# Five first slices of 128, 128, 256, 256 and 256 features, rows loaded by ACT at once and turned between the tiles of x, first weights in two blocks and three pairs

## The chip, the cores and the metric

The kernel runs on one NeuronCore of a Trainium2 chip, in fp32. The time is that of one launch on the device in microseconds; the figure for a kernel is the median of its runs. The engines are PE (TensorE, matrix products and transposes), DVE (VectorE), ACT (ScalarE), POOL (GpSimd) and SP (SyncE, which here only issues transfers).

## What is computed

One decoder layer on a sequence of 512 tokens and 1024 features. The change touches its first steps only:

```python
mod = silu(c) @ w_ada + b_ada                  # c: 1024, w_ada: 1024 x 6144
shift1, scale1, gate1, shift2, scale2, gate2 = split(mod, 6)
h = rms_norm(x, norm1_g) * (1 + scale1) + shift1
proj = h @ w_in                                # 1024 -> q, k, v, qi, ki, wi, u_pool, g_attn, g_pool
# then: indexer scores (qi, ki, wi), the 128 best keys of each query, attention with ALiBi over them,
# a causal pooling mixer, both gated and merged, @ w_out, added to x;
# then the second norm, modulated, @ w_up, a causal convolution of width 3 (conv_w, conv_b), silu gate, @ w_down
```

## The kernel before

Every matrix product in fp32 is made of three products of rounded parts: the operand is split into a high part (fp32r) and a low part (the rest), and PE adds high x high, high x low and low x high into one bank of PSUM. ACT makes high parts (`high_parts`, L788), DVE or POOL the low parts of weights (`low_parts`, L1209 on DVE in the first phase, L704 on POOL afterwards). Each engine runs a list written out by hand and waits on semaphores; nothing reorders it.

The first phase needs h transposed (features on partitions), in eight blocks k of 128 features, each 128 x 512 tokens. It goes so:

- SP issues the four tiles of x (L627), eleven small loads of rows (biases, gains, convolution taps, L630 to L637), then in turn for each of four slices of 256 features the part of w_ada for shift1 and scale1 (`load_first`, tiles ada_first0 to 3, four loads of 512 KB each with pieces of 1 KB) and the rows of w_in for the same two blocks k (`load_item`, tiles stage). Then come eight loads ada_row of 512 KB for shift2, and the weights of v.
- ACT loads c, takes silu(c) and then for each tile of tokens the sum of squares and the root (L805, L808). DVE takes the reciprocal and scales x into xn (L1240). PE turns xn in 128 x 128 pieces into all eight banks (L1613). ACT and DVE copy the banks to xT (four each).
- PE then sums slice 0 of mod with matmuls of c against ada_first (`first_sums`, L1627, into the eighth bank OB), ACT copies the four partial rows (L816), PE turns them into columns with matmuls against ones (`first_columns`, L1635), DVE adds the bias from the turned rows (`first_vectors`, L1217 to L1222), makes h of a block (full1, L1252), ACT its high part (L820), DVE its low part (L1229) and the low part of the weights (L1209). The rows and taps are turned on PE in one go between the sums and the columns of slice 0 (L1652 to L1655).
- PE does for each block k seven products of high x high, seven of h's low part and seven of the weights' low part (`first_products`, L1645), into seven banks that stay open over all eight blocks: qi (two), ki and wi (kw), q (four). The sums of the next slice stand behind the first block of a slice and its columns within the second.
- DVE accumulates the eight rows of macc_rows (the shift of the second norm; `mod_row_of`, L1171 and L1174) in two groups: five behind slice 2 and three behind slice 3. Only then come the low parts of qiT and kiT (L1261), which the first products of the indexer on PE wait for (`index_dots`, L1706), and then the indexer sums and fifteen rounds that find the best keys (L1309, L1312), up to kraw (L1351), for which the first attention scores on PE wait (L1827).

Of the kernel before, what the change touches and what calls it, by code (L numbers as in the profile page):

```python
# [62 lines left out]
ROW_LOADS = 11  # L63
# [8 lines left out]
KQ = KD // 2  # L72
THREE = ((0, 0), (0, 1), (1, 0))
# [40 lines left out]
class Schedule:  # L114
# [38 lines left out]
    def first(self):  # L153

        for q in range(KQ):
            self.items.append(("first", "in", (C_Q, C_QI), 2 * q, 2 * q + 2, 1))
            self.last_use.append(None)
            for r in range(2):
                self.units.append((1, r, KS))
                self.house()  # L160
                self.item_of.append(q)
                self.last_use[q] = ("unit", len(self.units))
        for at, name in enumerate(FIRST):
            self.opens(name, "dve", FIRST_BANK[at])
        self.ring = NBANK - 1
# [89 lines left out]
def build_layer(nc, x, c, w_ada, b_ada, norm1_g, w_in, q_norm_g, k_norm_g, w_attn_br, w_pool_grp, pool_scale,  # L255
# [17 lines left out]
    with ExitStack() as ctx:  # L273
# [53 lines left out]
        xn = place("xn", [P, NT, D], F32, hT_at)  # L327
# [3 lines left out]
        ada_first = [arena(f"ada_first{q}", [P, KD, S], F32, (16, 32, 62, 89)[q]) for q in range(KQ)]  # L331
# [78 lines left out]
        rows_in = sem("rows_in")  # L410
        x_in = [sem(f"x_in{t}") for t in range(NT)]
# [4 lines left out]
        ada_in = [[sem(f"ada_in{q}_{half}") for half in range(2)] for q in range(KQ)]  # L416
# [13 lines left out]
        c_t = sem("c_t")  # L430
        c_silu = sem("c_silu")
        c_pad = sem("c_pad")
        x_sum = sem("x_sum")
        x_t = sem("x_t")
        x_kept = [sem("x_kept_even"), sem("x_kept_odd")]
# [155 lines left out]
        def _(sp):  # L591
            def load_item(n):
# [5 lines left out]
                if kind == "first":  # L598
                    for c0, wide, c in FIRST_COLUMNS:
                        sp.dma_start(slot[:, 0:2 * KS].rearrange("p (k n) -> p k n", n=KS)[:, :, c:c + wide],  # L600
# [27 lines left out]
            for r, src in ((V_ADA, b_ada), (V_NORM1, norm1_g), (V_NORM2, norm2_g), (V_POOL, pool_scale)):  # L628
                v = src[0].rearrange("(k p) -> k p", p=P)
                sp.dma_start(rows[r:r + v.shape[0], 0, :], v).then_inc(rows_in, 16)  # L630
            for r, src in ((V_Q, q_norm_g), (V_K, k_norm_g)):
                for half in range(2):
                    sp.dma_start(rows[r:r + 1, 0, half * HD:(half + 1) * HD], src).then_inc(rows_in, 16)
            taps = conv_w[0].rearrange("j (m p) -> (j m) p", p=P)
            sp.dma_start(rows[:, 1, :], taps[0:P, :]).then_inc(rows_in, 16)
            sp.dma_start(rows[0:TAPS * 2 * KF - P, 2, :], taps[P:TAPS * 2 * KF, :]).then_inc(rows_in, 16)
            sp.dma_start(rows[TAPS * 2 * KF - P:(TAPS + 1) * 2 * KF - P, 2, :],  # L637
                          conv_b[0].rearrange("(m p) -> m p", p=P)).then_inc(rows_in, 16)
            def load_row(k):

                if k % 4 == 0:
                    sp.wait_ge(sums_ok, k // 4 + 1)
                sp.dma_start(ada_row[k][:, :], ada[:, k, 3 * D:4 * D]).then_inc(ada_row_in[k], 16)

            for n, item in enumerate(sch.items):
                if n < KQ:
                    load_first(n)
                if n == KQ + 4:
                    sp.wait_ge(sums_ok, KQ - 1)
# [7 lines left out]
                if n == KQ - 1:  # L657
# [115 lines left out]
        def _(act):  # L773
# [29 lines left out]
            for t in range(NT):  # L803
                act.wait_ge(x_in[t], 16)
                me.did(act.activation(junk[:, t % 2, :], xtok[:, t, :], ACT.Square,  # L805
                                      accum_out=tstat[:, 0, t:t + 1]), x_sum)
# [1164 lines left out]
```

## Time and profile before

| what | us |
|---|---|
| median of three runs | 735.16 |
| lowest, highest | 735.04, 736.5 |
| the profiled execution | 735.97 |
| its span, first to last instruction | 734.1 |
| PE busy | 717.5 |
| DVE, ACT, POOL busy | 382.5, 307.7, 299.8 |

The page of the profile gives the busy time of each engine and a chain of the work that ended last. The views used below are: the busy time of each engine in stretches of the span, with the clock granted to TensorE (1.00 is 2.4 GHz, 0.50 is 1.2 GHz) and the share and rate of the DMA engines; the waits; the chain; and the timeline, in which consecutive instructions of one line are merged with their count.

### The profile page before, as it was taken

To read this page: it belongs to the slowest core of one execution; us is meant where nothing else is said; L and a number is where in the kernel's file an instruction comes from. 1 tells how busy PE (TensorE), PEld (TensorE's weight loads), DVE (VectorE), ACT (ScalarE), POOL (GpSimd) and SP (SyncE) were. 2 spreads that over 40 slices of the span, in tenths; PEclk is the share of its full clock that TensorE was granted. 3 is DMA by queue.
4 is the path that set the end of the run, shared out by engine and by line. 5 is a ranking of instruction groups with operands and counts; after the bars stand their busy time and mean duration, and the time that the engine had idled before them with its cause. 6 is when DMAs were issued, how large, how long until landed. Compare 5 with 4: busy or idle time off the path is not lost.

```text
span 734.1 us, 9316 instructions
## 1 busy us (share of the span) xinstructions
PE 717.5 (98%) x3440; PEld 577.4 (79%) x3440; DVE 382.5 (52%) x706; ACT 307.7 (42%) x507; POOL 299.8 (41%) x159
## 2 busy tenths in 40 slices
PE   5899999999999999999999999999999999999997
PEld 3667688877776778887898888887888888888886
DVE  3458899964375506788955444545443432004002
ACT  6316532567577633352636334344334333121120
POOL 1001448826232325574315434434444434435440
PEclk9899999999999999999999999999999999999999
DMA  9993321311231226486095243244243233042401
GB/s 317 357 392 115 108 80 58 115 58 59 69 103 53 64 66 258 164 307 208 1 315 151 81 115 105 68 115 114 58 116 96 76 114 114 31 144 86 144 0 58
DMA packets 87306, 92.73 MB, mean 126 GB/s; under 512 B 2275, under 2 KB 69599, under 8 KB 87263
## 3 DMA queue, kind: packets, MB, share of 16 engines
q1 hardware_dynamic: 84927, 83.23, 35.5%
q10 hardware_dynamic: 2336, 8.92, 3.3%
q8 instruction: 28, 0.46, 0.3%
q14 instruction: 15, 0.12, 0.1%
HBM read 90.05 MB, written 2.10 MB: 126 GB/s over the span
## 4 chain that ended last, share of the span: by engine, by line
PE 81%; DVE 14%; ACT 1%; DMA 1%; SPq 1%; issue 1%; DVEq 0%; ACTq 0%
PE bank L1575 33%; PE bank L1595 21%; PE bank L1584 16%; PE bank L1645 4%; DVE work L1312 3%; DVE top L1309 3%; PE bank L1839 1%; PE bank L1827 1%; PE bank L1807 1%; DMA ada_first<-in_w_ada_dram 1%; PE bank L1627 1%; DVE macc_rows L1174 1%; DVE full L1490 1%; DVE pmean L1343 1%; DVE pmean L1339 1%
## 5 line engine op out<-in xcount | busy, mean ns | idle before, releaser
L704 POOL TENSOR_TENSOR wsplit<-stage,wsplit 128x1024 fp32r<-128x1024 f32 (+1 forms) x113 | 259.3, 2297 | 387.3 <-ACT wsplit L788 328.0
L1575 PE MATMUL bank<-hT,wsplit 128*128 128x512 f32 (+1 forms) x1120 | 257.5, 382 | 0.4 <-DVE hT L1498 0.4
L1575 PEld LDWEIGHTS bank<-hT,wsplit 128*128 128x128 f32 x1120 | 203.0, 188 | 41.9 <-issue 1.7
L788 ACT ACTIVATE wsplit<-stage 128x1024 fp32r<-128x1024 f32 (+2 forms) x121 | 120.0, 994 | 249.8 <-PE bank L1584 165.2
L1584 PE MATMUL bank<-hT,wsplit 128*128 128x512 f32 (+1 forms) x560 | 134.6, 382 | 0.0
L1595 PE MATMUL bank<-wsplit,guT 128*128 128x512 f32 x528 | 119.8, 389 | 0.0
L1584 PEld LDWEIGHTS bank<-hT,wsplit 128*128 128x128 f32 x560 | 101.5, 188 | 19.9 <-POOL wsplit L704 0.3
L1595 PEld LDWEIGHTS bank<-wsplit,guT 128*128 128x128 f32 x528 | 99.1, 188 | 20.6
L1533 DVE SCALAR_TENSOR_TENSOR yb<-bank,conv,yb 128x511 f32<-128x511 f32 (+1 forms) x44 | 33.0, 749 | 65.1 <-ACT yb L1108 64.3
L1533 DVE SCALAR_TENSOR_TENSOR ya<-bank,conv,ya 128x511 f32<-128x511 f32 (+1 forms) x44 | 33.0, 750 | 59.6 <-ACT ya L1108 58.8
L1458 DVE TENSOR_TENSOR tmp_last<-bank,gate_row 128x512 f32<-128x512 f32 x8 | 5.5, 688 | 101.7 <-PE bank L1595 101.7
L1645 PE MATMUL bank<-hT,wsplit 128*128 128x512 f32 x168 | 42.4, 410 | 2.0 <-ACT hT L820 2.0
L1645 PEld LDWEIGHTS bank<-hT,wsplit 128*128 128x128 f32 x168 | 32.7, 198 | 11.3 <-issue 4.5
L1402 DVE CUSTOM_DVE_ANT_0 logit<-logit,bank 128x128 f32<-128x128 f32 (+3 forms) x32 | 15.4, 482 | 37.8 <-PE bank L1827 35.9
L993 ACT ACTIVATE prob<-logit,sbias,stat 128x128 f32<-128x128 f32 (+3 forms) x32 | 20.9, 652 | 29.0 <-DVE sbias L1406 16.0
L1595 PE MATMUL bank<-wsplit,hT 128*128 128x512 f32 x96 | 24.1, 400 | 0.0
L1312 DVE MATCH_REPLACE8 work<-top,work 128x256 f32<-128x256 f32 (+2 forms) x45 | 24.0, 543 | 0.0
L1595 PE MATMUL bank<-wsplit,merged 128*128 128x512 f32 x96 | 22.5, 394 | 0.0
L1309 DVE MAX8 top<-work 128x8 f32<-128x256 f32 (+2 forms) x45 | 22.2, 549 | 0.5
L1595 PE MATMUL bank<-own,merged 128*128 128x512 f32 x96 | 22.5, 391 | 0.0
L1595 PEld LDWEIGHTS bank<-wsplit,hT 128*128 128x128 f32 x96 | 17.4, 188 | 5.7 <-issue 1.7
L1595 PEld LDWEIGHTS bank<-wsplit,merged 128*128 128x128 f32 x96 | 18.0, 188 | 4.2 <-issue 0.5
(193 smaller groups left out, 754.3 us busy)
## 6 DMA issues: line engine op xcount, KB each, us to landing
stage<-in_w_up_dram SPq DMA_DIRECT2D x44, 512.0 KB, 5.2
stage<-in_w_in_dram SPq DMA_DIRECT2D x14, 1024.0 KB, 5.2
stage<-in_w_down_dram SPq DMA_DIRECT2D x10, 1024.0 KB, 5.0
ada_first<-in_w_ada_dram SPq DMA_DIRECT2D x16, 512.0 KB, 9.5
ada_mid<-in_w_ada_dram ACTq DMA_DIRECT2D x8, 1024.0 KB, 7.9
ada_row<-in_w_ada_dram SPq DMA_DIRECT2D x8, 512.0 KB, 11.3
stage<-in_w_out_dram SPq DMA_DIRECT2D x4, 1024.0 KB, 7.2
ada_last<-in_w_ada_dram SPq DMA_DIRECT2D x4, 1024.0 KB, 11.0
```

Source lines behind the costliest of these rows:

```text
L704: pool.tensor_tensor(unit_split(n, 1), unit_source(n), unit_split(n, 0).bitcast(F32), ALU.subtract).then_inc(low, 1)
L788: me.did(act.activation(unit_split(n, 0), unit_source(n), ACT.Copy), high)
L993: me.did(act.activation(prob[:, t % 3, 0:n], logit[:, t % 2, 0:n], ACT.Exp, bias=sbias[:, t:t + 1], scale=stat[:, 2, r:r + 1], accum_out=s ...
L1174: me.did(dve.scalar_tensor_tensor(out=acc[:, :], in0=row, scalar=csil[:, k:k + 1], in1=acc[:, :], op0=ALU.mult, op1=ALU.add), mod_sum)
L1309: found = [me.did(dve.max(top8[:, i, :], row_of(src, i))) for i in range(1, NT)]
L1312: me.did(dve.match_replace(out=row_of(work, i), in_to_replace=top8[:, i, :], in_values=row_of(src, i), imm_value=TAKEN))
L1402: me.did(dve.tensor_tensor_reduce(logit[:, t % 2, 0:n], logit[:, t % 2, 0:n], SC[t % 2][:, 0:n], 1.0, TAKEN, ALU.add, ALU.max, smax[:, t:t ...
L1533: me.did(dve.scalar_tensor_tensor(out=y[:, m % 2, back:], in0=bank((kind, m))[:, 0:S - back], scalar=w, in1=y[:, m % 2, back:], op0=ALU.mu ...
L1575: pe.matmul(out_bank[:, tokens], hi[:, k, :], rhs[:, part, k, tokens], start=k == 0 and part == 0, stop=False)
L1584: mm = pe.matmul(out_bank[:, tokens], lo[:, k, :], rhs[:, 0, k, tokens], start=False, stop=k == nk - 1)
L1595: mm = pe.matmul(out_bank[:, :], rows_of[:, a, k0 + r, t * P:(t + 1) * P], unit_split(n, b)[:, r, :], start=first and r == 0 and (a, b) == ...
L1645: mm = pe.matmul(bank(name)[:, :], unit_split(k, a)[:, 0, at:at + P], hT[:, part, k, :], start=start, stop=stop)
```

## The change

- The first phase has five slices of 1, 1, 2, 2 and 2 blocks of 128 features. The two narrow slices load 512 KB for shift1 and 512 KB for scale1 in pieces of 512 bytes, with one semaphore. The weights come as blocks 0 and 1 alone and then three pairs.
- The short rows are loaded by ACT's queue (six loads, ahead of all its work), the taps by SP behind block 1's weights. PE turns the short rows into OB between the second and the third tile of x, and DVE copies them between its third and fourth tile; the taps are turned behind block 1 and copied by DVE in slice 2.
- PE makes sixteen transposes of ident at the start. It turns only seven blocks of each tile into banks and makes the sums of slice 0 before the last tile; the eighth block is turned into OB by `last_turn`, after slice 0's columns have been used. xn moves to the place of the fourth slice's tile, so SP waits for `last_t` before it loads that.
- DVE takes the squares of tile 1 in one pass and copies c out of PSUM; ACT's silu reads that copy. Block 0 of h is made from PSUM directly. The copies of banks are dealt out in another order around the first block, and the first products wait for the bank copies one by one (`LATE`).
- The rows of macc_rows are accumulated in groups of four and four.

The core of the diff:

```diff
-ROW_LOADS = 11
+ROW_LOADS, TAP_LOADS = 6, 3
+EARLY = (("qi", 0), ("qi", 1), ("kw", 0), ("q", 1), ("q", 2), ("q", 3), ("q", 0))
...
+WIDE = (1, 1, 2, 2, 2)
+NQ = len(WIDE)
+AT = tuple(sum(WIDE[:q]) for q in range(NQ))
+SLICE_OF = tuple(q for q in range(NQ) for _ in range(WIDE[q]))
+LATE = {("q", 2): (1, 2), ("q", 3): (0, 3), ("q", 0): (1, 3)}
+LOADS = ((0, 1), (1, 2), (2, 4), (4, 6), (6, 8))
...
-        for q in range(KQ):
-            self.items.append(("first", "in", (C_Q, C_QI), 2 * q, 2 * q + 2, 1))
+        for n, (k0, k1) in enumerate(LOADS):
+            self.items.append(("first", "in", (C_Q, C_QI), k0, k1, 1))
             self.last_use.append(None)
-            for r in range(2):
+            for r in range(k1 - k0):
                 self.units.append((1, r, KS))
                 self.house()
-                self.item_of.append(q)
-                self.last_use[q] = ("unit", len(self.units))
+                self.item_of.append(n)
+                self.last_use[n] = ("unit", len(self.units))
...
-        xn = place("xn", [P, NT, D], F32, hT_at)
+        xn = arena("xn", [P, NT, D], F32, 62)
...
             def load_first(q):
 
+                wide = WIDE[q] * P
+                if AT[q] == 4:
+                    sp.wait_ge(last_t, 1)
+                if WIDE[q] == 1:
+                    for j in range(2):
+                        c0 = j * D + AT[q] * P
+                        sp.dma_start(ada_first[q][:, :, j * P:(j + 1) * P], ada[:, :, c0:c0 + P]
+                                     ).then_inc(ada_in[q][0], 16)
+                    return
                 for half in range(2):
                     ks = slice(half * KQ, (half + 1) * KQ)
                     for j in range(2):
-                        c0 = j * D + 2 * q * P
-                        sp.dma_start(ada_first[q][:, ks, 2 * j * P:2 * (j + 1) * P], ada[:, ks, c0:c0 + 2 * P]
+                        c0 = j * D + AT[q] * P
+                        sp.dma_start(ada_first[q][:, ks, j * wide:(j + 1) * wide], ada[:, ks, c0:c0 + wide]
...
+                if item[0] == "first" and item[4] - item[3] > 1 and item[3] + 1 in AT:
+                    load_first(AT.index(item[3] + 1))
+                if n == 1:
+                    load_taps()
...
-            act.wait_ge(consts, 4)
+            for r, src in ((V_ADA, b_ada), (V_NORM1, norm1_g), (V_NORM2, norm2_g), (V_POOL, pool_scale)):
+                v = src[0].rearrange("(k p) -> k p", p=P)
+                act.dma_start(rows[r:r + v.shape[0], 0, :], v).then_inc(rows_in, 16)
+            for r, src in ((V_Q, q_norm_g), (V_K, k_norm_g)):
+                act.dma_start(rows[r:r + 1, 0, :].rearrange("p (a d) -> p a d", a=2),
+                              src.unsqueeze(1).to_broadcast([1, 2, HD])).then_inc(rows_in, 16)
+            act.wait_ge(consts, 5)
             me.did(act.activation(tstat[:, 2, 1:2], ones[:, 0:1], ACT.Silu))
-            act.wait_ge(c_t, 1)
-            me.did(act.activation(csil[:, :], banks[2][:, 0:KD], ACT.Silu), c_silu)
+            act.wait_ge(c_kept, 1)
...
+            token_squares(0)
+            token_roots(0, 1)
+            act.wait_ge(x_square, 1)
+            token_roots(1, 2)
+            token_squares(2)
+            token_roots(2, 3)
+            token_squares(3)
+            token_roots(3, 4)
...
+            row_sum(0)
             act.wait_ge(x_t, NT)
-            for k in range(0, KD, 2):
-                me.did(act.activation(xT[:, k, :], banks[k][:, :], ACT.Copy), x_kept[0])
-            for q in range(KQ):
-                act.wait_ge(sums_ok, q + 1)
-                me.did(act.activation(rowsum[:, :], OB[:, :], ACT.Copy), row_ok)
-                high_parts(2 * q + 1)
-                for k in (2 * q, 2 * q + 1):
-                    act.wait_ge(n_ok, k + 1)
-                    me.did(act.activation(hT[:, 0, k, :], full1[:, k % 2, :], ACT.Copy), h_hi)
-                high_parts(2 * q + 2)
+            x_copy(4)
+            x_copy(2)
+            high_parts(1)
+            h_high(0)
+            x_copy(6)
+            act.wait_ge(last_t, 1)
+            me.did(act.activation(xT[:, KD - 1, :], OB[:, :], ACT.Copy), last_kept)
+            for q in range(1, NQ):
+                row_sum(q)
+                for k in range(AT[q], AT[q] + WIDE[q]):
+                    high_parts(k + 1)
+                    h_high(k)
...
+            dve.wait_ge(c_t, 1)
+            me.did(copy_of(csil[:, :], banks[2][:, 0:KD]), c_kept)
+            dve.wait_ge(consts, 13)
+            me.did(dve.reciprocal(invn[:, :], invn[:, :]))
             dve.wait_ge(c_silu, 1)
-            dve.wait_ge(consts, 13)
             me.did(copy_of(cpad[:, :, 0], csil[:, :]), c_pad)
-            me.did(dve.reciprocal(invn[:, :], invn[:, :]))
+            dve.wait_ge(x_in[1], 16)
+            me.did(dve.tensor_tensor_reduce(junk[:, 1, :], xtok[:, 1, :], xtok[:, 1, :], 1.0, 0.0, ALU.mult, ALU.add,
+                                            tstat[:, 0, 1:2]), x_square)
             for t in range(NT):
                 dve.wait_ge(root_ok, t + 1)
                 me.did(dve.reciprocal(tstat[:, 3, t:t + 1], tstat[:, 2, t:t + 1]))
                 me.settle()
                 me.did(dve.tensor_scalar(xn[:, t, :], xtok[:, t, :], tstat[:, 3, t:t + 1], None, ALU.mult), xn_ok)
+                if t == 2:
+                    vectors()
+            def x_copy(k):
+                me.did(copy_of(xT[:, k, :], banks[k][:, :]), x_kept[1])
+
             dve.wait_ge(x_t, NT)
-            for k in (KD - 1, 1, 3, 5):
-                me.did(copy_of(xT[:, k, :], banks[k][:, :]), x_kept[1])
-            vectors()
-            for q in range(KQ):
+            x_copy(3)
+            first_vectors(0)
+            first_full(0)
+            x_copy(5)
+            x_copy(1)
+            first_low(0)
+            low_parts(1)
+            for q in range(1, NQ):
                 first_vectors(q)
-                for k in (2 * q, 2 * q + 1):
-                    if k % 2 == 0:
-                        dve.wait_ge(x_kept[0], k // 2 + 1)
-                    if k >= 2:
-                        dve.wait_ge(h_lo, k - 1)
-                    me.did(dve.tensor_scalar(full1[:, k % 2, :], xT[:, k, :], gs[:, 0, k:k + 1], mod[:, k:k + 1],
-                                             ALU.mult, ALU.add), n_ok)
-                for k in (2 * q, 2 * q + 1):
+                ks = range(AT[q], AT[q] + WIDE[q])
+                for k in ks:
+                    first_full(k)
+                if q == 2:
+                    tap_vectors()
+                for k in ks:
                     first_low(k)
                     low_parts(k + 1)
-                for k in ((), (), (0, 1, 2, 3, 4), (5, 6, 7))[q]:
+                for k in {4: (0, 1, 2, 3), 6: (4, 5, 6, 7)}.get(AT[q], ()):
...
+            for _ in range(16):
+                pe.transpose(banks[7][:, 0:P], ident[:, :], ident[:, :])
+            def row_turn():
+
+                pe.wait_ge(rows_in, 16 * ROW_LOADS)
+                pe.transpose(OB[:, 0:V_END], rows[0:V_END, 0, :], ident[0:V_END, 0:V_END]).then_inc(rows_t, 1)
+
+            def tap_turn():
+
+                pe.wait_ge(taps_in, 16 * TAP_LOADS)
+                pe.wait_ge(first_mod, 3)
+                pe.transpose(OB[:, 0:P], rows[:, 1, :], ident[:, :])
+                left = (TAPS + 1) * 2 * KF - P
+                pe.transpose(OB[:, P:P + left], rows[0:left, 2, :], ident[0:left, 0:left]).then_inc(taps_t, 1)
+
+            def last_turn():
+
+                pe.wait_ge(first_mod, 1)
+                for t in range(NT):
+                    mm = pe.transpose(OB[:, t * P:(t + 1) * P], xn[:, t, (KD - 1) * P:KD * P], ident[:, :])
+                mm.then_inc(last_t, 1)
...
+            pe.wait_ge(c_kept, 1)
+            for t in range(NT):
+                pe.wait_ge(xn_ok, t + 1)
+                if t == 2:
+                    row_turn()
+                if t == NT - 1:
+                    first_sums(0)
+                for k in range(KD - 1):
+                    mm = pe.transpose(banks[k][:, t * P:(t + 1) * P], xn[:, t, k * P:(k + 1) * P], ident[:, :])
+                mm.then_inc(x_t, 1)
+
             first_columns(0)
-            pe.wait_ge(vecs, 1)
-            for n in range(2):
-                pe.wait_ge(x_kept[n], KD // 2)
+            last_turn()
+            pe.wait_ge(x_kept[0], 2)
+            pe.wait_ge(x_kept[1], 1)
             for k in range(KD - 1):
-                first_products(k, h_hi, 0, 0, start=k == 0)
-                if k % 2:
-                    first_columns(k // 2 + 1)
+                q, after = SLICE_OF[k], SLICE_OF[k + 1]
+                if k and WIDE[q] == 1:
+                    first_sums(after)
+                first_products(k, h_hi, 0, 0, EARLY, start=k == 0)
+                if k == 0:
+                    first_sums(after)
+                elif after != q:
+                    first_columns(after)
                 first_products(k, h_lo, 1, 0)
+                if k == 0:
+                    first_columns(after)
+                if k == 1:
+                    tap_turn()
                 first_products(k, h_hi, 0, 1).then_inc(used, 1)
-                if k % 2 == 0 and k < KD - 2:
-                    first_sums(k // 2 + 1)
+                if WIDE[q] == 2 and k == AT[q] and q + 1 < NQ:
+                    first_sums(q + 1)
```

## Rows read from the trace of the kernel before

**Rows 1.** The page, busy time of PE over the span, share and count.

```profile
PE 717.5 (98%) x3440; PEld 577.4 (79%) x3440; DVE 382.5 (52%) x706; ACT 307.7 (42%) x507; POOL 299.8 (41%) x159
```

**Rows 2.** Windows: stretch, length, busy time of each engine, PE clock, DMA share, GB/s.

```profile
0.00:20.70 20.70, 9.62 (x60) 7.28 (x61) 8.76 (x24) 12.96 (x25) 2.73 (x17) 0.96 0.95 321
20.70:66.00 45.30, 45.27 (x222) 33.53 (x223) 26.22 (x38) 12.51 (x18) 3.27 (x1) 0.94 0.92 323
```

**Rows 3.** Waits of PE from 66 us on: total us, times, longest.

```profile
PE bank L1706 <- DVE kiT L1261: 0.5, 1, 0.5
PE bank L1827 <- DVE kraw L1351: 0.4, 1, 0.4
```

**Rows 4.** DVE: its timeline at 57 to 69 us, and macc_rows' passes in ns.

```profile
57.64 0.16 DVE L1217 TENSOR_TENSOR mod<-bank,vec 128x2 f32<-128x2 f32 x1 [1.27 <-PE bank L1635]
...
62.56 6.00 DVE L1174 SCALAR_TENSOR_TENSOR macc_rows<-ada_row,csil,macc_rows 128x1024 f32<-128x1024 f32 x3
...
L1174 DVE SCALAR_TENSOR_TENSOR macc_rows<-ada_row,csil,macc_rows x7: 1278/1285/3230, 50.9 to 67.3; 128x1024 f32<-128x1024 f32 x7
```

**Rows 5.** The chain that ended last, 8 to 41 us: start, length, what.

```profile
8.03 7.86 DMA ada_first<-in_w_ada_dram
...
19.84 0.64 ACT hT L820
...
20.73 7.37 PE bank L1645 x21
28.09 1.85 PE bank L1627 x16
...
31.78 0.79 PE bank L1635 x8
32.56 8.05 PE bank L1645 x35
```

**Rows 6.** Timeline of SP, ACT, DVE and PE from 1 to 19 us.

```profile
1.36 1.28 ACT L799 ACT_TABLE_LOAD   x1 [1.36 <-PEq L1958]
...
2.58 0.52 SPq L630 DMA_DIRECT2D rows<-in_b_ada_dram  x1
...
5.41 1.04 ACT L805 ACTIVATE junk<-xtok 128x1024 f32<-128x1024 f32 x1
...
6.78 1.04 ACT L805 ACTIVATE junk<-xtok 128x1024 f32<-128x1024 f32 x1
...
7.10 0.75 DVE L1240 TENSOR_SCALAR xn<-xtok,tstat 128x1024 f32<-128x1024 f32 x1
...
8.00 5.66 PE L1613 MATMUL bank<-ident,xn 128*128 128x128 f32 x32 [4.22 <-DVE xn L1240]
...
13.70 2.06 ACT L813 ACTIVATE xT<-bank 128x512 f32<-128x512 f32 x4 [2.73 <-PE bank L1613]
...
18.35 0.95 ACT L788 ACTIVATE wsplit<-stage 128x896 fp32r<-128x896 f32 x1 [0.69 <-DMA stage<-in_w_in_dram]
```

**Rows 7.** Issues: ada_first1's last, its us to landing, ACT's of ada_mid in ns.

```profile
14.56 1.71 SPq L619 DMA_DIRECT2D ada_first<-in_w_ada_dram  x1
...
ada_first<-in_w_ada_dram SPq DMA_DIRECT2D x1, 512.0 KB, 9.8
...
L1025 ACTq DMA_DIRECT2D ada_mid<-in_w_ada_dram x8: 374/394/482, 273.2 to 328.7; - x8
```

**Rows 8.** Windows as rows 2: first phase, then loads of w_up in 512-byte pieces.

```profile
18.00:20.00 2.00, 0.77 (x7) 0.68 (x7) 1.37 (x7) 1.11 (x2) 0.00 (x0) 0.72 1.10 346
20.00:24.00 4.00, 3.27 (x8) 2.63 (x9) 3.56 (x5) 1.83 (x3) 0.00 (x0) 0.50 1.09 360
24.00:28.00 4.00, 4.00 (x15) 2.94 (x13) 0.00 (x0) 0.00 (x0) 0.00 (x0) 0.79 1.08 357
...
457.00:458.00 1.00, 1.00 (x6) 0.84 (x5) 0.00 (x0) 1.00 (x2) 0.44 (x1) 1.00 1.11 332
458.00:459.00 1.00, 1.00 (x6) 0.84 (x5) 0.78 (x2) 0.67 (x2) 1.00 (x1) 1.00 1.14 315
```

More of the change, by code:

```diff
@@ L415, in build_layer @@
         ada_last_in = [sem(f"ada_last_in{q}") for q in range(KD // 2)]
-        ada_in = [[sem(f"ada_in{q}_{half}") for half in range(2)] for q in range(KQ)]
+        ada_in = [[sem(f"ada_in{q}_{half}") for half in range(2)] for q in range(NQ)]
         stage_in = [sem(f"stage_in{n}") for n in range(NSTAGE)]
@@ L434, in build_layer @@
         x_t = sem("x_t")
+        vec_ok = sem("vec_ok")
+        last_t = sem("last_t")
+        last_kept = sem("last_kept")
         x_kept = [sem("x_kept_even"), sem("x_kept_odd")]
@@ L627, in _, with load_taps @@
                 sp.dma_start(xtok[:, t, :], x[0, t * P:(t + 1) * P, :]).then_inc(x_in[t], 16)
[L628 to L638, printed above, removed]
+            def load_taps():
+                taps = conv_w[0].rearrange("j (m p) -> (j m) p", p=P)
+                sp.dma_start(rows[:, 1, :], taps[0:P, :]).then_inc(taps_in, 16)
+                sp.dma_start(rows[0:TAPS * 2 * KF - P, 2, :], taps[P:TAPS * 2 * KF, :]).then_inc(taps_in, 16)
+                sp.dma_start(rows[TAPS * 2 * KF - P:(TAPS + 1) * 2 * KF - P, 2, :],
+                              conv_b[0].rearrange("(m p) -> m p", p=P)).then_inc(taps_in, 16)
             def load_row(k):
                 if k % 4 == 0:
-                    sp.wait_ge(sums_ok, k // 4 + 1)
+                    sp.wait_ge(sums_ok, SLICE_OF[k // 2 + 1] + 1)
                 sp.dma_start(ada_row[k][:, :], ada[:, k, 3 * D:4 * D]).then_inc(ada_row_in[k], 16)
             for n, item in enumerate(sch.items):
[L646 to L649, printed above, removed]
+                if item[0] == "first" and item[3] in AT:
+                    load_first(AT.index(item[3]))
+                if n == len(LOADS) + 4:
+                    sp.wait_ge(sums_ok, SLICE_OF[5] + 1)
                     sp.dma_start(wgrp[:, :, :], w_pool_grp[0].rearrange("g c d -> c g d")).then_inc(wgrp_in, 16)
@@ L807, in _, with token_roots @@
                 me.settle()
[L808 removed]
+            def token_roots(t0, t1):
+                me.did(act.activation(tstat[:, 2, t0:t1], tstat[:, 0, t0:t1], ACT.Sqrt, bias=eps[:, 0:1],
                                       scale=1.0 / D), root_ok)
[L811 to L813 removed]
@@ L1633, in first_columns @@
                 pe.wait_ge(row_ok, q + 1)
-                for n in range(4):
+                for n in range(2 * WIDE[q]):
                     mm = pe.matmul(OB[:, MC + n:MC + n + 1], rowsum[:, n * P:(n + 1) * P], ones[:, 0:1],
@@ L1644, in first_products @@
                     at = FIRST_AT[FIRST.index(name)]
+                    if start and name in LATE:
+                        pe.wait_ge(x_kept[LATE[name][0]], LATE[name][1])
                     mm = pe.matmul(bank(name)[:, :], unit_split(k, a)[:, 0, at:at + P], hT[:, part, k, :],
```

87 lines of the change are left out of this document (53 added, 34 removed).

## The prediction

> **What bounds the kernel now.** I read the page's busy shares first, then the busy time by stretches, then what PE waited for, then the start as a timeline. PE is busy 98% of the span, with 717.5 us of work [rows 1]. The windows show where the rest lies: before 20.7 us PE is busy 9.62 us of 20.70, and in the next 45.3 us it idles 0.03 us [rows 2]. So the start is the one large hole, and any other gain must be PE work that goes away. After 66 us PE waits only twice before the heads: 0.5 us on DVE's low part of kiT and 0.4 us on DVE's kraw [rows 3]. Between these two DVE is never free for long (the sorting rounds), so from the last columns of the first phase (57.64 us) up to the kraw wait there are two nearly equal bounds, PE and DVE [rows 4]. What is added to DVE there moves the end; what is taken from PE there alone does not.
>
> The start is a chain in three parts. SP issues four loads of x, eleven of rows and taps, and only then ada_first0. Its last quarter is issued at 8.03 and lands 7.86 us later, at 15.89, and the products begin at 20.73 [rows 5]. The DMA engines are full at 346 to 360 GB/s in the windows from 18 to 28 us [rows 8], so bytes ahead of a transfer count, not the moment of its issue. TensorE's granted clock is 0.72, 0.50 and 0.79 in the windows from 18 to 28 us: it is at 1.2 GHz for some 5 us of the first products, and 21 of them take 7.37 us where 35 later take 8.05 us (0.23 us each). At 0.23 they would have taken 4.8, so the low clock costs 2.5 us here [rows 5, 8].
>
> **Part 1: when the first products start.** Ahead of ada_first0 stand x and now only the short rows; the slice itself is 1 MB and not 2. One MB less at 357 GB/s is -2.9 us, and the taps behind it another -0.25. Its pieces are 512 bytes instead of 1 KB. The nearest rows of such pieces are the loads of w_up: 332 and 315 GB/s with the engines full, against 360 [rows 8]. That makes 1 MB slower by 0.3 us (ends: 0.1 by 332 against 346, 0.4 by 315 against 360). Landing: 15.89 - 2.9 - 0.25 + 0.3 = 13.0 us. The Trainium skill (DMA: Bandwidth & Descriptors, Specifications) puts line rate at pieces from 512 bytes on; by it the 0.3 us would be nothing. The rows shown differ by about a tenth, and the rows decide.
>
> ACT pays for the six row loads. It issues them at 0.37 to 0.48 us each [rows 7]; on SP one took 0.52 us [rows 6]. At 0.4 and 0.04 between them that is 2.6 us before its first table load, which ran at 1.36 and now runs at about 3.97. The short Silu, the c one and the Sqrt table follow in the same order as before, so the first square goes from 5.41 to about 6.97 us (+1.6). DVE takes over one square (I price it by the 1.28 us of a two-input DVE pass over 1024 columns [rows 4]; it lies beside ACT's table loads), so ACT has three squares at steps of 1.37 us [rows 6], not four. Xn of the first tile ends at 9.4 instead of 7.85, and PE turns it from 9.5 us at 0.21 us each, as its first ones run now [rows 6], to 11.0; tile 1 to 12.2, rows 12.5, tile 2 13.3. DVE's vector copy between xn2 and xn3 waits for that turn of the rows; behind it stands xn3, which ends near 14.0. PE does the sums of slice 0 from 13.3 (landed 13.0): four column groups of half the width, 0.93 us by half of 1.85 [rows 5], to 14.2, then the last tile, 7 transposes, to 15.3. ACT then needs two copies of xT at 0.52, the weights' high part at 0.95 and h's high part at 0.64 [rows 5, 6]; with the 0.25 us that PE took after that before, products start at **18.15** instead of 20.73: 2.6 us earlier. DVE's branch (a copy, the vectors, the first full) is shorter than ACT's, and the xT copies that fell out of this chain must only be ready 1 us later, for the fourth to seventh product. The sixteen transposes of ident run from 3.8 to 7.2 while PE would idle and cost nothing.
>
> **Part 2: from there to the sums of slice 2.** PE does 21 products (3 x 1.61), the new half sums of slice 1 (0.93) and two new columns (half of 0.79 [rows 5]): 18.15 + 4.83 + 0.93 + 0.40 = 24.3 us. Ada_first2 ends where ada_first1 ends now, since the bytes ahead are the same: 14.56 + 9.8 = 24.36 [rows 7], plus 0.3 for each of the two narrow slices, 25.0; its first half is there earlier. The sums end at the later of 24.3 + 1.85 = 26.15 and 25.0 + 0.93 = 25.9. So PE and DMA are about even here: a later PE costs fully, an earlier one would bring nothing. Before, the corresponding sums end at 28.09 + 1.85 = 29.94. Gain 3.8 us at full clock. What follows (products of k = 1 and 2, sums, columns) is the same list, plus the turn of the taps, two transposes with a wait, 0.4 us (0.2 to 0.8, by the columns' 0.79). SP waits for last_t before slice 3, at about 17 us; it reaches that wait only at 19 or so and has some 9 us of transfers queued behind it, so nothing runs dry. ACT's and DVE's shorter steps lie beside 1.6 us blocks of products.
>
> **Part 3: DVE after the last columns.** The eight rows of macc_rows are now split 4 and 4, not 5 and 3. The fourth in the last group is one more pass of 1.28 us, 1.35 with the gap behind it (three passes of 1.28, 3.23 and 1.28 take 6.00 [rows 4]), between the last low part and qiT. Nothing hides it: PE already waits 0.5 us there on kiT [rows 3, 4], and DVE is the second bound until kraw. It costs 1.35 us. The row taken from the earlier group gives nothing back, as DVE idled there before the last columns anyway. One of the three present passes takes 3.23 us; the fourth comes in addition, so I let this stand.
>
> **The sum.** -3.8 + 0.4 + 1.35 = -2.05 us with TensorE at full clock as the first products run. If it runs at 1.2 GHz for as long as now, 2.5 us come back: +0.45. Now PE does sparse work for 7 us, from the last tile's turn to the products (13.7 to 20.7 [rows 5, 6]), and the clock falls within them; after the change it is sparse for 3 (15.3 to 18.15), with four transposes in it. The rows show no gap of that size, so both ends stay, and I take the middle, half the present loss: -2.05 + 1.25 = **-0.8 us**. The profiled run is 735.97 us, 734.1 of it span, and the median of the runs is 735.16; against the median the forecast is **734.4 us** (profiled 735.2).
>
> **Rivals.**
> First, the clock stays at 2.4 GHz. For it: the gap is less than half as long and holds dense work. Against it: the present trace falls to the lower level although PE's waiting before 20.7 us is broken up by work at many places (it is busy for 9.62 us [rows 2]). Time 733.1. The Trainium skill (TensorE: Matmul & The Clock Gate, What's actually happening) calls the throttled state the default that activity releases. By that rule, too, the shorter gap would help; it leaves open which case holds.
>
> Second, the low clock lasts as long as now: 735.6 us. This is no change, as what a measurement tells apart here is about 0.2%, 1.5 us.
>
> Third, slower: PE's new order puts the sums of slice 0 ahead of the last tile. If ada_first0 lands late, everything of x waits. Every us past 13.3 then moves the start of the products one us. With the clock low it gives a slower kernel (over 1.5 us) from a landing at 14.4; at 15.9, as now, the start is where it was, and the additions 0.93 + 0.4 + 0.4 + 1.35 make 738.2. For it: xn3 stands behind the rows' turn as well, and ACT's issues are a guess from 1 MB loads. Against it: a whole MB less lies ahead.
>
> Fourth, the extra pass on DVE does not show, because DVE's other passes there get shorter (the one of 3.23 us has 1.95 us to give): 1.3 us less than each case, 733.1 with the middle clock.
>
> **How the numbers follow.** Forecast (-0.8 +/- 0.7) 0.38; clock full 0.22; clock as long as now 0.12; late start 0.16; DVE pass hidden 0.12. Faster by over 0.2% (under 733.7): the second and last of these and a little of the forecast, 0.36. Slower by over 0.2% (over 736.6): the late start and the upper tail, 0.18. Within: 0.46. The range goes from 732.6 (full clock with half of the DVE cost gone) to 736.9 (low clock and a landing a us late).
>
> **What would show it.** Ada_first0's last landing near 13.0 and the products' first start near 18.15; a first square of ACT near 7; the sums of slice 2 ending near 26 and not over 27.5; the last columns some 2 to 3.4 us before 57.6; four macc passes behind them and a PE wait on kiT of 1.8 instead of 0.5 us; the same 0.4 us wait on kraw. The granted clock between 15 and 26 us tells the first two rivals apart. I am wrong if 512-byte pieces land much slower, if ACT's issues are not some 0.4 us, or if DVE between 57 and 163 us has slack that the waits don't show.

## The result: slower by 0.2%, and the profile after

The changed kernel took 737.04 us (median of 13 runs, 735.43 to 739.9), the kernel before 735.87 beside it: a ratio of 1.0021, 95% interval 1.0013 to 1.0029, or 1.0 to 2.1 us more. The prediction was 734.4 us with a range of 732.6 to 736.9, counted from the median of 735.16 of the three runs known then. The profiled execution of the changed kernel took 736.43 us (span 734.6).

The page's first line and the waits of PE over the whole span (total us, times, longest), to be read beside [rows 1, 3]:

```profile
PE 719.8 (98%) x3472; PEld 579.6 (79%) x3472; DVE 383.3 (52%) x711; ACT 306.5 (42%) x506; POOL 299.2 (41%) x159
...
PE bank L1765 <- DVE xn L1316: 2.4, 1, 2.4
PE bank L1827 <- DVE kiT L1344: 1.9, 1, 1.9
PE bank L1753 <- ACT hT L858: 1.3, 1, 1.3
PE bank L1711 <- DVE mod L1279: 0.6, 1, 0.6
...
PE bank L1948 <- DVE kraw L1434: 0.3, 1, 0.3
```

The wait on kiT has grown from 0.5 to 1.9 us and the one on kraw is still there. The chain that ended last, as in [rows 5]:

```profile
9.75 3.22 PE bank L1765 x14
12.97 0.12 PE bank L1697
13.09 1.49 PE bank L1765 x7
14.58 1.37 PE bank L1733 x16
15.96 0.93 PE bank L1765 x7
16.89 0.02 issue
16.91 1.08 ACT xT L854 x2
18.00 0.84 ACT wsplit L813
18.83 0.61 ACT hT L858
19.45 0.25 issue
19.69 1.84 PE bank L1753 x7
21.53 1.00 PE bank L1733 x16
...
26.41 1.85 PE bank L1733 x16
...
39.45 1.85 PE bank L1733 x16
```

PE works without a break from 9.75 to 16.89 us, turning x (L1765), the rows (L1697) and summing slice 0 (L1733). The first 21 turns are slow (seven take 1.49 us), the last seven take 0.93: the rate goes up within the sums of slice 0. This is read from the lengths of the instructions. The granted clock of the profile says 1.00 all the time (columns as in [rows 2]); but in changed_53_first_filled's profile, where it says 0.50, seven turns take the same 1.49 us, so the slow rate is that of 1.2 GHz.

```profile
9.70:15.30 5.60, 5.55 (x30) 4.86 (x34) 2.79 (x7) 1.78 (x6) 0.00 (x0) 1.00 1.16 311
```

So a clock of 1.00 in the column, or in the mean of a run, doesn't show that the first turns ran at the full rate. Below, "slow turns" means this rate, in whatever way the column reads. The products (L1753) start at 19.69, not 20.73 as before, and the sums of slice 2 at 26.41, not 28.09. The timelines of ACT at the start and of DVE behind the last columns, as in [rows 4, 6]:

```profile
4.14 1.28 ACT L830 ACT_TABLE_LOAD   x1 [4.14 <-issue]
...
7.16 1.04 ACT L837 ACTIVATE junk<-xtok 128x1024 f32<-128x1024 f32 x1
...
56.48 0.16 DVE L1278 TENSOR_TENSOR mod<-bank,vec 128x2 f32<-128x2 f32 x1 [2.24 <-PE bank L1741]
...
61.41 7.39 DVE L1235 SCALAR_TENSOR_TENSOR macc_rows<-ada_row,csil,macc_rows 128x1024 f32<-128x1024 f32 x4
```

The last columns come at 56.48, 1.16 us sooner than before, and the four passes take 7.39 us against 6.00 for three: 1.39 more. So the indexer starts at 71.48 us and not 71.25. The lead of the start is gone there. (From there to the end the profile loses another 0.3 us: its span is 0.5 us longer. Where isn't settled.)

Issues of ada_first0's last load and ada_first2's last, with us to landing, as in [rows 7]:

```profile
3.12 1.32 SPq L636 DMA_DIRECT2D ada_first<-in_w_ada_dram  x1
ada_first<-in_w_ada_dram SPq DMA_DIRECT2D x1, 512.0 KB, 9.6
...
17.10 0.79 SPq L643 DMA_DIRECT2D ada_first<-in_w_ada_dram  x1
ada_first<-in_w_ada_dram SPq DMA_DIRECT2D x1, 512.0 KB, 8.0
```

They land at 12.7 and 25.1 us; 13.0 and 25.0 were forecast.

### The profile page after: what moved, and what is told of

Same layout as the page of the kernel before. It is cut to its first block, busy times and chain, and to the rows that moved or that the text cites. A ratio compares the mean times of both kernels' runs of the same rounds, so it can differ in the third digit from the quotient of the medians.

```text
span 734.6 us, 9386 instructions
## 1 busy us (share of the span) xinstructions
PE 719.8 (98%) x3472; PEld 579.6 (79%) x3472; DVE 383.3 (52%) x711; ACT 306.5 (42%) x506; POOL 299.2 (41%) x159
## 4 chain that ended last, share of the span: by engine, by line
PE 82%; DVE 14%; ACT 2%; issue 1%; ACTq 0%; DVEq 0%
PE bank L1658 33%; PE bank L1678 21%; PE bank L1667 16%; PE bank L1753 4%; DVE work L1395 3%; DVE top L1392 3%; PE bank L1960 1%; PE bank L1948 1%; PE bank L1928 1%; PE bank L1733 1%; DVE macc_rows L1235 1%; PE bank L1765 1%; DVE full L1573 1%; DVE pmean L1426 1%; DVE pmean L1422 1%
## 5 line engine op out<-in xcount | busy, mean ns | idle before, releaser
L1753 PE MATMUL bank<-hT,wsplit 128*128 128x512 f32 x168 | 40.9, 396 | 1.3 <-ACT hT L858 1.3
L1753 PEld LDWEIGHTS bank<-hT,wsplit 128*128 128x128 f32 x168 | 30.8, 188 | 10.5 <-issue 4.4
```

Source lines behind the costliest of these rows:

```text
L1753: mm = pe.matmul(bank(name)[:, :], unit_split(k, a)[:, 0, at:at + P], hT[:, part, k, :], start=start, stop=stop)
```

## The experiments

All ratios are to the kernel before, run on the same chip beside each, on several chips in all; the interval is some 0.1% to either side, 0.7 us, so differences between two of them are sure to about 1 us.

| kernel | median us (runs) | ratio, 95% interval |
|---|---|---|
| the change | 737.04 (13) | 1.0021 (1.0013 to 1.0029) |
| macc_5_3 | 735.10 (11) | 0.9994 (0.9985 to 1.0002) |
| rows_on_sp | 736.99 (12) | 1.0020 (1.0010 to 1.0030) |
| idents_28 | 737.67 (8) | 1.0028 (1.0017 to 1.0039) |
| no_idents | 737.57 (11) | 1.0026 (1.0018 to 1.0035) |
| before_macc_4_4 | 737.87 (5) | 1.0030 (1.0018 to 1.0042) |
| before_macc_6_2 | 736.53 (11) | 1.0008 (0.9999 to 1.0017) |
| rows_sp_macc_5_3 | 734.62 (12) | 0.9982 (0.9973 to 0.9992) |
| rows_sp_53_idents_22 | 733.67 (12) | 0.9976 (0.9965 to 0.9987) |
| kit_filled | 736.49 (12) | 1.0010 (1.0001 to 1.0018) |
| pairs_rows_sp_53 | 737.89 (12) | 1.0020 (1.0004 to 1.0036) |
| rows_sp_53_first_filled | 733.82 (11) | 0.9978 (0.9968 to 0.9989) |
| before_first_filled | 733.43 (5) | 0.9965 (0.9953 to 0.9977) |
| changed_both_filled | 735.85 (11) | 1.0005 (0.9996 to 1.0014) |
| changed_53_first_filled | 734.39 (11) | 0.9981 (0.9972 to 0.9990) |
| before_44_both_filled | 734.97 (11) | 0.9990 (0.9981 to 0.9999) |

### The pass on DVE

```diff
-                for k in {4: (0, 1, 2, 3), 6: (4, 5, 6, 7)}.get(AT[q], ()):
+                for k in {4: (0, 1, 2, 3, 4), 6: (5, 6, 7)}.get(AT[q], ()):
```

> The changed kernel with macc_rows' rows in groups of five and three, as before. Theory 1 (the fourth pass on DVE sets the indexer's start): PE's wait on kiT falls from 1.9 to about 0.5 us, and the time falls by 1.4 us against the changed kernel (737.04 median), to some 735.6. Rival (DVE has slack behind the first phase, as the time is set by PE's work): no change within 0.4 us, although the wait on kiT gets shorter.

The wait on kiT is 0.5 us again and 0.0027 of the time (2.0 us) is gone, 0.6 us more than the pass lasts, which is within what such a difference is sure to. The rest of the change is then level with the kernel before. The other way round, the kernel before with groups of four and four:

> The kernel before with nothing changed but macc_rows' rows in groups of four and four. Theory 1: PE's wait on kiT grows from 0.5 to 1.9 us and the time by 1.4 us; in runs where that wait is followed by a low clock (as in the profile of rows_on_sp, at 71.4 us) by up to 1.7 us more, so 1.4 to 2.2 in the median. Rival (it was the new start, not the pass, that costs; the pass was only seen in the wait): less than 0.5 us.

It is 2.2 us slower than before, again more than the pass. In its profiled execution the chain shows a further loss behind the wait:

```profile
71.53 0.62 PE bank L1706 x4
72.15 2.45 PE bank L1595 x6
...
78.10 1.60 PE bank L1595 x6
```

Six products take 2.45 us behind the wait and 1.60 us later: the granted clock is 0.50 from about 72.6 to 76 us, which costs 1.5 us against the same list in the kernel before. Six and two rows do not help:

> The kernel before with groups of six and two. DVE idled 1.27 us before the last columns, a pass takes 1.35, so the last slice's vectors come at most 0.1 us later. Theory 1: the wait on kiT (0.5 us) goes, and DVE starts the indexer up to 0.5 us earlier: 0.3 to 0.5 us shorter than before. Rival (a row of ada_row has not landed, the DVE group is longer than the gap): the last slice's first products wait, and the time is the same or longer.

The expected gain of 0.3 to 0.5 us did not come. The wait on kiT by DVE falls only from 0.5 to 0.3 us, since ACT's part of kiT is ready at 69.56 us and two steps of DVE follow it; the first products of the indexer start at 71.04 instead of 71.25. The 0.0008 more lies within its interval of none.

### ACT's issues and the turns of x

```diff
-                act.dma_start(rows[r:r + v.shape[0], 0, :], v).then_inc(rows_in, 16)
+                sp.dma_start(rows[r:r + v.shape[0], 0, :], v).then_inc(rows_in, 16)
...
```

All six row loads move, to between the loads of x and ada_first0.

> The changed kernel with the six row loads issued by SP between x and ada_first0, ACT's queue free of them. Theory 2 (ACT's issues delay the squares and all of x): ACT's first square goes from 7.16 back to about 5.4 us, the first turn of x from 9.75 to about 8.1, and the products' start from 19.69 to 18.2 to 18.6 us, as ada_first0 lands near 13; time 1.1 to 1.5 us shorter than the changed kernel. Rival (bytes and the landing of ada_first0 set the start): it lands 1 to 2 us later, because SP issues it 2 us later, and the start stays within 0.4 us of 19.69.

In the profile the products start at 17.18 us, 2.5 earlier, but not by ACT's issues alone: in this execution 14 turns take 1.75 us, so the slow turns are gone as well. Four profiles part the two. With the rows on ACT the products start at 19.69 (slow turns, the changed kernel) or 17.82 (fast turns, idents_28, shown below), with the rows on SP at 17.82 (slow turns, rows_sp_macc_5_3) or 17.18 (fast turns, here). ACT's six issues thus cost 1.9 us with slow turns and 0.6 with fast turns, and the slow turns 1.9 us in the changed kernel. The time of rows_on_sp is that of the changed kernel, though, where 1.1 to 1.5 us less was expected. The rival fails too: ada_first0 lands at 12.25 us, not later. The windows (columns as in [rows 2]) behind the wait on kiT, which ends at 70.37 here:

```profile
66.00:70.37 4.37, 2.49 (x14) 1.78 (x12) 4.20 (x7) 3.48 (x7) 0.00 (x0) 1.00 0.01 2
70.37:71.40 1.03, 1.03 (x8) 0.85 (x9) 1.03 (x2) 0.38 (x2) 0.00 (x0) 1.00 0.00 0
71.40:74.80 3.40, 3.40 (x13) 2.23 (x12) 1.90 (x5) 1.72 (x6) 0.00 (x0) 0.50 0.00 0
```

PE had been busy for 2.49 of 4.37 us, and TensorE then runs at 1.2 GHz from 71.4 to 74.8 us; the first seven products were at 1.2 GHz too (3.25 us against 1.84 in the changed kernel). That costs 1.5 us (from the start of the indexer to the end of its third block, 8.15 us against 6.66) and 1.4. In the changed kernel's own profile neither happened, but its median is 0.6 us above that profile and its runs reach 739.9.

```diff
-            for _ in range(16):
+            for _ in range(28):
                 pe.transpose(banks[7][:, 0:P], ident[:, :], ident[:, :])
```

> The changed kernel with 28 transposes of ident at the start, not 16, so that PE works without a break until xn0 is there. Theory 3 (PE turns x at 1.2 GHz and its chain from 9.75 to 16.88 us sets the start): the granted clock is 2.4 GHz for these, a tile of seven takes about 1.0 and not 1.6 us, the sums of slice 0 0.9 and not 1.4 us, and the products start 1.2 to 1.8 us earlier; time down by as much, and the spread of the runs smaller. Rival (xn3 and the landing of ada_first0 set the start, the clock only looks like it): the start moves by under 0.4 us. If PE is still busy with idents when xn0 is there, up to 0.5 us are lost.

The chain of its profile:

```profile
9.73 1.75 PE bank L1765 x14
...
13.02 1.07 PE bank L1733 x16
...
17.82 1.85 PE bank L1753 x7
...
24.54 1.85 PE bank L1733 x16
```

Fourteen turns in 1.75 us, not 3.22, and the products at 17.82, 1.87 sooner: in this execution the slow turns are gone, and it took 734.56 us, 1.87 less than the changed kernel's profiled one. That the slow turns set the start is thus seen in one pair of executions. That more idents take them away isn't shown: rows_on_sp had fast turns with sixteen, and the median here is no better than the change's. The other seven runs took 736.2 to 738.05, with a mean clock of 0.994 to 0.998. They have no profile; where their clock was low isn't settled.

> The changed kernel without the sixteen transposes of ident. If they help the clock (theory 3, weak form): the first turns are at 1.2 GHz all the same, as PE idles from 7.4 to 9.7 us in between, so no change within 0.3 us in the profile; in the timed runs up to 0.5 us longer in the median. Rival (the idents keep the clock up in a good part of the runs): 1 us or more longer.

0.0005 more than the change, which the intervals don't tell from nothing. Its profile has the same slow turns (3.22 us for 14), so the sixteen transposes do not bring the rate up there.

### Rows on SP and five and three together

> The changed kernel with the six row loads on SP and groups of five and three. The profile of rows_on_sp had its products start at 17.18 us, 2.5 earlier than the changed kernel, at a low clock up to 20.2, and lost 1.7 us to a low clock behind the wait on kiT. Theory 4 (a PE wait of 1.9 us on kiT lets the clock fall in part of the runs; with 0.5 us it does not): all runs keep 2.4 GHz at 71 us, and the time is 2 to 3 us below rows_on_sp (736.99), 734 to 735, below before. Rival (the low clock there is chance and not tied to the wait): only the 1.4 us of the pass.

2.8 us less than rows_on_sp by the ratios, where the pass explains 1.4; the rest is more than the 1 us such a difference is sure to, but barely, so theory 4 is favoured and not shown. Its slowest run but one is 735.31, and it is faster than the kernel before. With 22 idents:

> The same with 22 transposes of ident, so that PE is at work from 3.7 to about 8.1 us, when the first xn is there. Theory 3 (idents up to the first turn bring 2.4 GHz for the turns of x): tiles of x at 1.0 us; but ada_first0's landing near 12.3 us then sets the start, so at most 0.5 us less than with 16. Rival (more work ahead keeps the clock up into the first products): 1 us or more less.

0.4 us less, in the noise. Its profiled run was its slowest (736.93): its turns before the sums of slice 0 were fast, but the granted clock was low from 14.2 to 24.5 us, so idents alone do not secure it.

### The narrow slices alone

Slices of 256 features and weights in pairs again, taps copied one slice sooner:

```diff
-WIDE = (1, 1, 2, 2, 2)
-LOADS = ((0, 1), (1, 2), (2, 4), (4, 6), (6, 8))
+WIDE = (2, 2, 2, 2)
+LOADS = ((0, 2), (2, 4), (4, 6), (6, 8))
```

> rows_sp_macc_5_3 with four slices of 256 features and weights in pairs again, all else as changed (turns, copies, idents). It tells what the narrow slices are worth alone. Theory 5 (they bring the first landing of ada_first0 some 3 us forward, from about 15.3 to 12.3, and cost 0.9 us of sums and 0.4 of columns): products start 2.5 to 3 us later than 17.2, sums of the slice behind 0.9 + 0.4 less, so 1.2 to 1.6 us slower than rows_sp_macc_5_3 (734.6). Rival (DMA sets the pace of slice 2 in either case, at about 25 us, so the early start is lost again): within 0.6 us of it.

2.8 us slower than rows_sp_macc_5_3 in the ratios, more than expected, with runs from 734.46 to 740.28. Its four fastest (to 735.13, clock 0.999 and more) lie 1.2 to 1.6 us above the four fastest of rows_sp_macc_5_3 (733.24 to 733.5), which is the price expected; the other eight have a clock of 0.989 to 0.997. The profile waits for ada_first0 (7.05 + 8.41 = 15.5 us) and starts products at 21.73. So narrow slices are worth an estimated 1.4 us where the rows are on SP; it rests on a choice of the fastest runs, on two chips.

### PE's waits filled

Ahead of the turn of wi, in the changed kernel:

```diff
+            for _ in range(14):
+                pe.transpose(OB[:, P:2 * P], ident[:, :], ident[:, :])
             wi_turn()
```

> The changed kernel (groups of four and four) with fourteen transposes of ident on PE ahead of the turn of wi, in the time in which PE waits 1.9 us for kiT. They compute nothing that is used. Theory 4 (the wait lets TensorE's clock fall in part of the runs): the pass of 1.35 us stays in the time, but the runs of over 739 us vanish and the median falls by 0.4 to 0.8 us, from 737.0 to some 736.4; the wait on kiT is then about 0.2 us. Rival (the excess over the pass comes from elsewhere): the median stays within 0.3 us, or grows by the transposes.

The ratio falls by 0.0011, 0.8 us, and no run is above 737.67, where the changed kernel had three, up to 739.9. The pass is still there. This is what theory 4 expects, that the wait costs clock besides its length, but 0.8 us is less than the 1 us to which two ratios can be told apart. What is shown is that a low clock can follow the wait: it did in the profiles of rows_on_sp and before_macc_4_4, for 1.5 us each, and not in that of the changed kernel. (In the fillers and idents nothing that PE computes is used.)

Before the first products, in the kernel before:

```diff
+            for _ in range(14):
+                pe.transpose(banks[3][:, 0:P], ident[:, :], ident[:, :])
             for k in range(KD - 1):
                 first_products(k, h_hi, 0, 0, start=k == 0)
```

> The kernel before with fourteen transposes of ident right before the first products, in PE's wait of 2.0 us. Theory 6: the clock falls at 18.9 us all the same in the runs that look as the profile does, but rises again one step sooner (from 25.7 to 22.3 us), so the median is 0.8 to 1.5 us shorter than before. Rival (the low clock is not shortened by them): within 0.3 us, or longer by up to 0.3 as the transposes at 1.2 GHz take 3 us and push the products.

2.6 us faster than before, the lowest median of all (the next ratio, 0.9976, lies within its interval), with a clock of 0.999 or more in all five runs. Windows, as in [rows 8], and chain:

```profile
18.00:20.00 2.00, 1.93 (x18) 1.69 (x17) 1.39 (x5) 1.45 (x3) 0.00 (x0) 1.00 1.10 348
20.00:24.00 4.00, 3.90 (x17) 3.25 (x18) 3.30 (x4) 1.42 (x3) 0.00 (x0) 1.00 1.09 361
```

```profile
20.10 5.05 PE bank L1645 x21
25.16 1.85 PE bank L1627 x16
```

The first 21 products take 5.05 us, not 7.37 [rows 5], and the sums behind them start at 25.16 us: 1.25 sooner than those of slice 2 in the changed kernel at 26.41, although that kernel's products start 0.4 us sooner. The expectation was too careful: the clock does not fall at the first products here.

> rows_sp_53_idents_22 with ten more transposes of ident right before the first products, where PE waits 1.2 us for h's high part. Theory 6 (the low clock in the first products comes from PE's idling between the last turn and them): fewer runs with the clock at 1.2 GHz there, median 0.5 to 1 us below 733.67; no delay, since the transposes end before h is there. Rival (the clock falls by what lies further back, or 1.2 us of transposes is too little): within 0.3 us of 733.67.

No gain over rows_sp_53_idents_22: here the rival holds. In its profile (span 731.8) the turns are fast, the granted clock is full and the sums of slice 2 wait for ada_first2, which lands at 25.6 us. Here the transfers set the order, not PE.

### Both sides with PE's waits filled

> The changed kernel with ten transposes of ident before the first products and fourteen in the wait on kiT. Theory 7 (at an equal, full clock the new start buys about nothing, since the transfers set the sums of slice 2, and the pass costs 1.4): 735.0 to 735.8 us, 1.6 to 2.3 above before_first_filled (733.43), and a spread under 1.5 us. Rival (the new order itself is faster by its 1.7 us in the profile): 733.5 to 734.2.

> The changed kernel with groups of five and three and ten transposes before the first products. Theory 7: the turns of x at 1.2 GHz still put the first products at 19.2 to 19.7 us, so 733.5 to 734.6, 0 to 1.2 us above before_first_filled. Rival (the start is worth what the prediction took, 3.8 us less 0.4 at full clock): below 732.

> The kernel before with fourteen transposes before the first products, groups of four and four and fourteen transposes in the wait on kiT. Theory 1 at full clock: the pass costs 1.4 us against before_first_filled, 734.6 to 735.0, and not 1.9 as in before_macc_4_4. Rival (the 0.5 us more was no matter of the clock): 735.3 or more.

Against before_first_filled (0.9965) the pass costs 0.0025 (1.8 us), the new start 0.0016 (1.2 us) and both 0.0040 (2.9 us). This is not yet an equal clock: in changed_both_filled's profile 14 turns of x take 3.01 us, on the chain. In the kernel before the turns are over by 13.7 us and the sums behind them wait for ada_first0 until 15.9, so slow turns cost it nothing.

The time of changed_53_first_filled falls as expected by theory 7, at the upper end, but in its profile not for the reason given: no transfer is waited for. Its products start at 18.52, 1.58 us before those of before_first_filled, and its sums of slice 2 at 25.23 against 25.16, since 1.65 us more work lies between; the taps and the gap for them make the next sums 0.5 us later again. As for the rest, changed_both_filled (735.85) and before_44_both_filled (734.97) are within or just beside their numbers. In the profile of the last the fourteen transposes before the products fell on a low clock, took 2.99 us instead of some 1.7 and pushed the products to 21.61: the price that filling can have.

## Why the prediction was wrong

**The step that failed** is the start of the products in part 1, 18.15 us: it priced PE's turns of x as if their rate went up after about a tile and a half. In the profile all three tiles ahead of the sums were slow and the products started at 19.69. This is 1.5 us, all of it ahead of the last turn of x, and more than the 1.3 us that the new order was to gain at an equal clock. The other misses are smaller.

**The profiled execution, term by term.** Its granted clock reads 1.00 to the end, so it is to be held against the forecast at full clock, 2.05 us less. It took 0.46 us more (736.43 against 735.97), 2.5 us off. Of this the late start is 1.54, the three blocks of products 0.54 (they took 5.37 us and were priced 4.83), the taps 0.1 and the half sums 0.1; some 0.3 us behind the start of the indexer has no explanation. idents_28's profile is the cross-check: with fast turns it started its products at 17.82, ended the sums of slice 2 at 26.39 (forecast 26.15) and took 734.56 us, 1.4 less than the kernel before. So the sum held but for 0.6 us where its condition was met, in one execution.

**Part 1, the start.** The landing (12.7 for 13.0) and ACT's issues (first table at 4.14 for 3.97, first square at 7.16 for 6.97) were right. The error is PE: I let tile 2 be turned by 13.3 and the last tile by 15.3 us, as if the rate went up near 12 us as in the profile of before. But ACT's six issues had moved the first turn from 8.0 to 9.75, and the rate went up only within the sums of slice 0, from 14.58 to 15.96: 21 slow turns, sums of slice 0 in 1.37 and not 0.93 us, the last turn at 16.9. I had checked the clock for the products alone, where the granted clock shows it. In the kernel before the slow turns hid behind the landing of ada_first0; the change put them on the chain.

**Part 2.** The terms behind the start were sized well but for the products: half sums 1.00 (0.93), columns 0.34 (0.40), sums to sums 13.04 us against 12.52 for the taps, 0.52 (0.4). The sums of slice 2 start at 26.41 for 24.3: 1.5 from the start, 0.5 from the products. They end at 28.26, past the 27.5 named as a sign of being wrong.

**Part 3.** The pass cost 1.39 us in the trace (1.35). What I missed is that the wait it makes can cost clock as well: 1.5 us in each of two profiles, nothing in the changed kernel's own, and 0.8 us, less than can be told apart, in kit_filled's comparison. I had listed the price of the wait, not what it can do to the engine that waits.

**The clock.** Of the forecast's 3.8 us, 2.5 were the low clock of the present start, and half of that was given back; so it counted 1.25 us for the clock and 1.3 for the order, less 0.4 and 1.35. In the medians filling PE's waits takes 2.6 us from the kernel before and 1.2 from the changed one, 1.4 apart: the term for the clock was about right. The one for the order was not. With PE's waits filled on both sides the new start is 1.2 us slower (each such number is sure to about 1 us), where 0.9 faster was forecast; the 2.9 us that both parts cost there, less the 1.4, are the 1.5 us measured (taken from the same ratios, so no check on them). Even with fast turns the new start gains little: idents_28's sums of slice 2 start 0.6 us before before_first_filled's, and the taps take 0.5 of it back. The rival of the late start named the added work (0.93 + 0.4 + 0.4 + 1.35) but tied it to a late landing. The bound by ada_first2 near 25 us stands, too: in two profiles with the rows on SP it is what the sums of slice 2 wait for.

The first rival (full clock, 733.1, which is 733.9 for a profiled run) fails with 736.43 us although the granted clock reads 1.00; what it left out are the slow turns. The second (the low clock lasts as long as now, 735.6) may fit more runs than the profile shows: seven of the thirteen list a mean clock of 0.994 or 0.995, as the kernel before's profile does with its 6.8 us at 1.2 GHz, and their times go from 736.98 to 739.9. None of them has a profile, but macc_5_3's, with the same start, has the granted clock at 0.50 from about 19.7 to 23 us: its first seven products take 2.90 us and the half sums behind them 1.50, 1.6 us more than in the changed kernel's profile. The fourth (hidden pass) is refuted by macc_5_3 and by the 7.39 us of the four passes.

Not settled: where the clock was low in the runs without a profile, and so 0.6 us between the changed kernel's profile and its median, and why more idents bring fast turns in a profile and no gain in the median.

## What to carry to other kernels

Before a start-up order is rebuilt to win 2 us, see which clock its products run at: here a few idle transposes before the first products brought 2.6 us, more than any new order. A gain that is counted against a stretch at the low clock contains the clock's part, and a new wait of PE of 2 us costs its length and may cost clock after it. Slow work that a later landing hides is free until a new order puts it on the chain: take its rate from the lengths of its instructions, not only from the granted clock. A step moved to another engine's idle time (rows to ACT) has to be followed to the engine that then starts later.

## What the runs showed of the hardware

How long SP is held at an issue depended on when it came there. In the timeline of the changed kernel the two loads of block 0's weights (256 KB and less) take 4.98 us to issue, behind the narrow slice in pieces of 512 bytes.

```profile
4.48 4.98 SPq L615 DMA_DIRECT2D stage<-in_w_in_dram  x2
9.51 1.81 SPq L636 DMA_DIRECT2D ada_first<-in_w_ada_dram  x2
```

The short pieces alone do not explain it: in rows_on_sp the same two loads behind the same slice take 2.49 us, from 6.71, so SP is free at 9.46 and 9.20 us. In the changed kernel it came 2.2 us sooner and waited 2.5 us longer. Nor did an earlier issue bring an earlier landing: ada_first0's last load, issued at 3.12 and 6.11 us, landed at 12.7 and 12.25.

TensorE's clock fell after one wait of 1.9 us in two executions (rows_on_sp, before_macc_4_4) and not in another of almost the same list, and the same 14 turns took 3.22, 3.01, 2.06 or 1.75 us in executions with much the same start. So a single profile prices neither a wait nor a start. And the granted clock read 1.00 over turns at the rate of 1.2 GHz, so it has to be read beside the lengths of known instructions.
